# Block-one attention: the softmax scaling of each probability tile moved from VectorE to ScalarE

## What is computed

```python
q, k, v = jnp.split(a_lat @ w_qkv, 3, axis=-1)          # kc, vc from a_ctx
s_lat = einsum('bnqhd,brnkhd->bhnqrk', qr, kb) + bias    # masked to a window
s_ctx = einsum('bnqhd,bchd->bhnqc', qr, kc)
p = jax.nn.softmax(concatenate([s_lat, s_ctx], -1), -1)
o = einsum(..., p_lat, vb) + einsum(..., p_ctx, vc)
y = o @ w_out
```

## Time and profile before

| | |
|---|---|
| time, median of 3 runs | 2984.95 us (2981.44 to 2986.52) |
| the profiled execution: its time, its span | 2987.08 us, 2985.8 us |
| TensorE busy, mean granted clock | 2828.6 us (95%), 0.97 |
| VectorE busy | 2008.2 us (67%) |
| ScalarE busy | 1226.4 us (41%) |
| attention loop of block one | from 987 us to 1134 us of the span |
| first row maxima of pairs 0 to 7 | at 992.85, 1011.70, 1030.16, 1048.29, 1066.23, 1084.35, 1102.49 and 1120.16 us |

### The profile page before, as it was taken

The page is one execution under the profiler, slowest core; times in us unless marked ns, Lnnn a source line. Parts: engine busy times, 40 slices in busy tenths (PEclk is TensorE's granted clock), DMA queues, the critical chain, the costliest instruction groups (busy, mean ns, idle before and its releaser), DMA issues.

```text
span 2985.8 us, 61177 instructions
## 1 busy us (share of the span) xinstructions
PE 2828.6 (95%) x26596; PEld 2675.9 (90%) x26596; DVE 2008.2 (67%) x2887; ACT 1226.4 (41%) x1633; POOL 336.9 (11%) x331
## 2 busy tenths in 40 slices
PE   7999998999999998998999989999999998999999
PEld 4888886999999877988999988999999998988998
DVE  4787686777776797677646765676565577647654
ACT  2222324444444334434544422455454444144643
POOL 5000001202001121004010020020020101000301
PEclk9999998999999998999998999999999999999999
DMA  7454353899996786998655622456576663233664
GB/s 272 124 173 156 117 166 114 224 256 279 257 270 194 209 246 184 265 289 218 183 162 153 165 62 86 114 169 179 166 194 168 172 169 101 87 105 114 178 166 131
DMA packets 747400, 525.15 MB, mean 176 GB/s; under 512 B 19370, under 2 KB 711788, under 8 KB 747004
## 3 DMA queue, kind: packets, MB, share of 16 engines
q1 hardware_dynamic: 743004, 516.18, 60.4%
q0 software_dynamic: 4128, 5.06, 0.6%
HBM read 520.07 MB, written 2.94 MB: 175 GB/s over the span
## 4 chain that ended last, share of the span: by engine, by line
PE 40%; DVE 9%; ACT 6%; issue 5%; DMA 1%; POOL 0%; DVEq 0%; SPq 0%; ACTq 0%; POOLq 0%
PE bank L497 11%; PE bank L499 11%; PE bank L498 11%; ACT weights_hi L467 4%; DVE weights_lo L477 2%; DVE conv_out L2304 1%; PE bank L2478 1%; PE bank L2470 1%; PE bank L2482 1%; PE bank L1453 1%; PE bank L526 1%; DMA weights_raw<-in_ffn_w 1%; DVE side_sums_odd L598 0%; DVE side_sums L598 0%; PE bank L1445 0%
## 5 line engine op out<-in xcount | busy, mean ns | idle before, releaser
L477 DVE TENSOR_TENSOR weights_lo<-weights_raw,weights_hi 128x2048 fp32r<-128x2048 f32 (+3 forms) x414 | 853.9, 2063 | 367.5 <-ACT weights_hi L467 367.2
L467 ACT ACTIVATE weights_hi<-weights_raw 128x2048 fp32r<-128x2048 f32 (+3 forms) x414 | 709.3, 1714 | 628.5 <-PE bank L499 498.9
L497 PE MATMUL bank<-ffn_in_hi,weights_hi 128*128 128x256 f32 x1184 | 343.9, 290 | 20.1 <-DVE ffn_in_lo L1223 10.5
L498 PE MATMUL bank<-ffn_in_lo,weights_hi 128*128 128x256 f32 x1184 | 338.9, 286 | 0.0
L499 PE MATMUL bank<-ffn_in_hi,weights_lo 128*128 128x256 f32 x1184 | 338.5, 286 | 0.0
L497 PE MATMUL bank<-mix_in_hi,weights_hi 128*128 128x256 f32 x960 | 284.2, 296 | 6.8 <-DVE mix_in_lo L1988 3.7
L497 PE MATMUL bank<-mac_in_hi,weights_hi 128*128 128x256 f32 x1024 | 288.7, 282 | 1.6 <-DVE mac_prod L2087 1.1
L499 PE MATMUL bank<-mac_in_hi,weights_lo 128*128 128x256 f32 x1024 | 289.8, 283 | 0.0
L498 PE MATMUL bank<-mac_in_lo,weights_hi 128*128 128x256 f32 x1024 | 289.4, 283 | 0.0
L498 PE MATMUL bank<-mix_in_lo,weights_hi 128*128 128x256 f32 x960 | 276.5, 288 | 0.0
L499 PE MATMUL bank<-mix_in_hi,weights_lo 128*128 128x256 f32 x960 | 276.1, 288 | 0.0
(11 more groups left out here) (434 smaller groups left out, 7017.7 us busy)
## 6 DMA issues: line engine op xcount, KB each, us to landing
weights_raw<-in_ffn_w SPq DMA_DIRECT2D x132, 512.0 KB, 6.4
weights_raw<-in_w_in SPq DMA_DIRECT2D x120, 512.0 KB, 5.1
side_weights<-in_ada_w SPq DMA_DIRECT2D x86, 576.0 KB, 4.4
weights_raw<-in_ffn_wg SPq DMA_DIRECT2D x88, 512.0 KB, 4.0
weights_raw<-in_ffn_wu SPq DMA_DIRECT2D x88, 512.0 KB, 5.3
weights_raw<-in_ffn_wd SPq DMA_DIRECT2D x64, 704.0 KB, 4.6
weights_raw<-in_ffn_w SPq DMA_DIRECT2D x48, 704.0 KB, 7.3
side_weights<-in_ada_w SPq DMA_DIRECT2D x112, 256.0 KB, 3.1
```

The costliest lines, as they stand in the source:

```text
L467: k.s.activation(k.w_hi[s % HIGHS][:, 0:n], k.raw[s % RING][:, 0:n], ACT.Copy).then_inc(*k.hi.up())
L477: k.v.tensor_tensor(k.w_lo[s % RING][:, 0:n], k.raw[s % RING][:, 0:n], k.w_hi[s % HIGHS][:, 0:n].bitcast(F32), ALU.subtract).then_inc(*k.l ...
L497: k.te.matmul(out, l[0], r[0], start=first, stop=False)
L498: k.te.matmul(out, l[0], r[1], start=False, stop=False)
```

## The change

For block one's attention the product of a tile with the reciprocal leaves VectorE and becomes an activation (`Identity` with a scale taken from `small`) on ScalarE. In ScalarE's list the normalisation of tile 0 stands behind the exponential of tile 1, that of tile 1 behind the exponential of tile 2, that of tile 2 behind the exponential of tile 3, and that of tile 3 last. VectorE keeps the four reciprocals. Block two is as before. No DMA and no buffer changes.

```diff
-        self.normed = k.sig("pair_normed", "dve")
+        self.normed = k.sig("pair_normed")
+        self.normed.engine = "act" if self.na else "dve"
...
+def act_normalise(k, m, n, i):
+    k.s.wait_ge(*m.inverted.at(4 * n + i + 1))
+    k.s.activation(k.pair_probs[i][:, 0:m.width(i % 2)], k.pair_probs[i][:, 0:m.width(i % 2)], ACT.Identity,
+                   scale=k.small[:, 24 + i:25 + i]).then_inc(*m.normed.up())
...
             s.activation(k.pair_probs[i][:, 0:w], k.AB[i][:, 0:w], ACT.Exp, bias=k.small[:, 20 + i:21 + i],
                          accum_out=k.small[:, 24 + i:25 + i]).then_inc(*m.exped.up())
+            if m.na and i:
+                act_normalise(k, m, n, i - 1)
+        if m.na:
+            act_normalise(k, m, n, 3)
...
             v.reciprocal(sums, sums).then_inc(*m.inverted.up())
+            if m.na:
+                continue
             v.wait_ge(*m.inverted.at(4 * n + i + 1))
```

## The result

| | before | after |
|---|---|---|
| median of 5 runs | 2984.95 us (2981.44 to 2989.28) | 2997.29 us (2995.37 to 3003.01) |
| profiled execution, its span | 2987.08, 2985.8 us | 3002.81, 3001.5 us |
| VectorE, ScalarE busy | 2008.2, 1226.4 us | 1995.3, 1247.2 us |
| first row maximum of pair 1 to that of pair 7 | 108.46 us | 123.58 us |

The change makes the kernel slower: by 12.3 us by the medians, a ratio of 1.0047 with an interval of 1.0033 to 1.0061. That is 0.3 us above the end of the range that was forecast (2997.29 against 2997.0).

A forecast was written before the change was run, and what follows sets the result against it. VectorE's work from R to the second copy of a transposed tile was taken to close the loop. 3.4 us (pairs 1 to 6) plus 1.6 (last pair) made 5.0, moving 2984.95 to 2990.0; range 2984.5 to 2997.0.

The forecast's parts named there:

- The steps to `weights_lo`: Each pair: exponentials 2 and 3 queue behind normalisations on ScalarE, so VectorE's `weights_lo` starts 0.57 us later than before.
- R: Start of a pair's first row maximum on VectorE; R+5.35 was forecast for `weights_lo`, R+4.78 before the change.
- p: Pace of one normalisation on ScalarE, taken as 0.61 us with bounds 0.51 and 0.71; `weights_lo` starts at R + 4.13 + 2p.
- the break-even at 0.33 us: Value of p below which `weights_lo` would start earlier than its old R+4.78.
- The direct sum: Attention stage: 6 x 0.57 = 3.4 us in pairs 1 to 6 plus 1.6 in the last, together 5.0 us slower.
- a rival, with a chance of 0.25: Attention stage: longer TensorE gaps make its clock fall; one fall gives 2993.0 us, two give 2996.0; chance 0.25.
- The prediction's own sign of failing: Attention stage: among the conditions under which the forecast fails, a clock below 1.00 in pairs 1 to 7.
- the upper bound that the prediction gave: Side pieces on VectorE stretched by GpSimd's mask addition, pairs 1 to 6: 6.5 us now, between 4.6 and 8.6 after.
- Pair 0: First pair of the stage: the 0.57 us delay costs nothing, or 0.57 if TensorE's lateness were gone.
- the cover: Pair 0: TensorE, its projection at the low clock, is 0.8 us later than VectorE, hiding the 0.57 us delay.
- The faster one: Attention loop keeps VectorE's saving because exponentials are not held up: net 5.9 us less, 2979.0 us; chance 0.08.

The follow-up runs named there:

- the two profiles where the clock was kept up: Changed kernel with fourteen unused TensorE products before the product with the values, 2990.64 us; the same plus six before each last-pair tile's transposes, 2992.03 us.
- the profile with fourteen products: Changed kernel plus fourteen unused TensorE products ahead of the product with the values, in pairs with a projection: 2990.64 us against 2985.39 before.
- the kernel with more of them in the last pair: Changed kernel with fourteen unused products, plus six before the transposes of each of the last pair's four tiles: 2992.03 us against 2984.48 before.
- the second profile: Changed kernel run again unaltered, beside the kernel before: 2997.12 us against 2984.48, ratio 1.0032; the profiled execution took 2999.45 us.
- The kernel with the smallest delay: Kernel before plus one unused 128x128 row maximum on VectorE per pair, ahead of `weights_lo`: 1.5 us above before, ratio 1.0004.
- the kernel with the largest delay: Kernel before plus two unused 128x512 row maxima on VectorE per pair, ahead of `weights_lo`: 15.0 us above before, ratio 1.0057.

## Why the prediction was wrong, point by point

**The steps to `weights_lo` held.** Predicted R+5.35, measured R+5.37 (5.43 where a side finish stands ahead of it). The pace of a normalisation was 0.61 to 0.63 (0.61 taken), VectorE idled behind reciprocals 1 and 2, no function table was loaded between. The steps held for the other orders too, with later values where ScalarE's slab ended late: with one normalisation ahead of exponential 3 R+4.29 to 4.86 (4.20 by the steps), with none R+3.62 to 4.10 in pairs 1 to 6 (3.62). No run varied p itself, so the break-even at 0.33 us is argued, not shown.

**The direct sum held.** Predicted 3.4 for pairs 1 to 6 and 1.6 for the last; 3.1 and 4.4 in the two profiles where the clock was kept up, and the last pair's 1.6 but for what the filler itself adds. By time: 5.3 and 7.5 us by the medians of the two kernels without falls in pairs 1 to 6, intervals 1.0015 to 1.0036 and 1.0010 to 1.0028; 5.0 us was said.

**What failed is the clock, as a term left out of the sum.** The sum of 5.0 us took the stage at full clock and put its falls at nothing. They were priced only as a rival, with a chance of 0.25, one or two falls and 3 us for each, because TensorE had kept 2.4 GHz through a gap of 2.38 us, and a gap of 2.95 us in pair 1 and the thin stretch of the last pair seemed the only new risks. The prediction's own sign of failing, a clock below 1.00 in pairs 1 to 7, is what the trace shows: 0.92 in each of pairs 1 to 6 and 0.88 in the last. There were six falls in pairs 1 to 6, at gaps of 2.10 to 2.97 us, each of them half as dear as was said: 9.7 us together, 1.6 a pair, read off as the time from the product with the values to the next R. The remainder agrees: of the 15.1 us that pairs 1 to 6 took longer, 3.1 are the direct part as in the profile with fourteen products, 2.0 are the side pieces stretched by the mask addition (8.5 us instead of 6.5, close to the upper bound that the prediction gave), and 10 are left. With fourteen products the stretching was 6.5 us again, in the kernel with more of them in the last pair some 1.4 us more, and that is the 4.4 against the 3.1. In the second profile pairs 1 to 6 had two falls, worth 2.9 us. By medians, 12.3 or 12.6 against 5.3 to 7.5 without falls, the clock is about half of what the change costs.

**Pair 0** was said to cost nothing, since TensorE was 0.8 us late there at the low clock. In the profiled execution that projection ran at full clock, the cover was gone, and the fall came behind the gap instead: 21.60 us from R to R, 18.85 before. In the second profile it was 20.19, again with a fall behind the gap. The cover was real in one execution and rested on a low clock, which the prediction itself had read off.

**The range** ended at 2997.0 because two falls were given less than a tenth. A slower outcome had 0.48 and the same 0.44; the likeliest value, 2990.0, was 7.3 us too low; it is close to what the mechanism costs with the clock held up (2990.64 and 2992.03).

**The rivals.** The faster one was right about its mechanism and wrong about this order: with no normalisation ahead of exponential 3, `weights_lo` does start 0.6 to 1.2 us earlier and the kernel gains 7.5 us (5.9 said), 10.2 with the last pair on VectorE. The Trainium skill's sentence on moving work to ScalarE when VectorE is saturated ("Perfetto Trace Analysis", "Optimizing Scalar/DVE Operations") thus comes out right here for one order of the instructions and wrong for another.

**Left open.** What decides whether a given gap makes the clock fall: see below. And the last pair: giving it back to VectorE regained nothing measurable in the changed kernel, where a stretch at 1.2 GHz stayed in it. With the normalisations last the gain went from 7.5 to 10.2 us, each against its own runs of before, and the clock of the pair from 0.88 to 1.00; but the two intervals meet (0.9968 to 0.9986 and 0.9960 to 0.9977), so this too is not shown by time.

## What to carry to other kernels

When work goes from a full engine to an idle one, write down the new order on the receiving engine and ask who waits for what now stands behind it: here two moved instructions of 0.6 us ahead of an exponential cost more than four of 0.4 us had saved, and behind it, in the pairs with a projection, nobody waited for them. Put the moved work where its result is needed, not where its input is ready, and treat a stretch in which nothing hides it (the last pass of a loop) by itself. And if a loop leaves TensorE a gap of two microseconds in every pass, price the clock as part of every delay, not as an accident; filling the gap with unused matmuls is a cheap test of it.

## What the runs showed of the hardware that was not expected

A longer gap is not by itself what makes the clock fall. The kernel with the smallest delay kept 2.4 GHz through a gap of 3.01 us in pair 1, with the product behind it at its full pace, and the changed kernel lost it behind 2.10. Within one execution of the kernel with the largest delay it was kept behind 2.91 us (pairs 2 and 5) and lost behind 2.58 and 2.92 (pairs 3 and 4):

```profile
1028.35 1.95 PE L1469 MATMUL bank<-hidden,na_v 128*64 128x256 f32 x16 [3.01 <-issue]
```

```profile
1067.27 2.95 PE L1469 MATMUL bank<-hidden,na_v 128*64 128x256 f32 x16 [2.58 <-issue]
...
1088.81 3.48 PE L1469 MATMUL bank<-hidden,na_v 128*64 128x256 f32 x16 [2.92 <-issue]
...
1110.24 1.95 PE L1469 MATMUL bank<-hidden,na_v 128*64 128x256 f32 x16 [2.91 <-issue]
```

The changed kernel itself had six falls in pairs 1 to 6 in one execution and two in another, with gaps of much the same size (2.10 to 2.97 and 1.73 to 2.98 us): a gap of 2.10 us stood before a fall in the first and before none in the second. In the first the falls came one pair apart each time, every 20.5 us. The Trainium skill's page "TensorE: Matmul & The Clock Gate" (section "Part 1: The HAM clock gate (the "warmup" mystery)") says that the gate's timing runs free of the kernel, so that how many matmuls are slow varies from run to run of one kernel. The two profiles of one kernel agree with the variation; that the gate's timing is its cause, no run here shows. Whether the period of the falls and the period of the loop held each other, as the even distance suggests, no run here was made to show.

Whether a cost that depends on the clock also widens the scatter of the times is not shown: the ten runs of the changed kernel reach over 10 us (2992.69 to 3003.01), but fifteen runs of the kernel before, on one chip, over 17 us (2978.13 to 2995.29).
